# Two chained transformer blocks on one core: gate base product spread over the last two experts, last weight strip in two transfers, memory query copy and compressed maximum reordered

## What is computed

```python
def expert_choice_ffn(h, w_router, w_gate, w_up, w_down):      # 16 experts, 32 rows each
    aff = softmax(h @ w_router);  gates, idx = top_k(aff.T, 32)
    xe = h[idx]
    ye = (silu(xe @ w_gate) * (xe @ w_up)) @ w_down
    return zeros_like(h).at[idx].add(ye * gates)

x = x + expert_choice_ffn(rms_norm(x, norm_ffn), w_router, w_gate, w_up, w_down)
g = sigmoid(rms_norm(x, norm_ple) @ w_ple_gate)
e = rms_norm(p @ w_ple_proj, norm_ple_post)
x = x + g * e
...
# second block, for each of four groups of heads (and, beside it, recurrence head and memory head g)
s = q @ kc.T * NSA_SCALE;  p = masked_softmax(s)               # compressed
s = qh @ k.T * MEM_SCALE;  p = softmax(s);  y_mem = p @ v      # memory
```

## Time and profile before

| | us |
|---|---|
| median of 3 runs | 1643.49 (1643.08 to 1643.61) |
| the profiled execution | 1643.12 |
| its span, first to last instruction | 1641.3 |
| TensorE busy | 1333.6 (81%) |
| VectorE busy | 517.7 (32%) |
| ScalarE busy | 187.1 (11%) |
| GpSimd busy | 41.1 (3%) |
| moved | 518.46 MB, mean 316 GB/s |

### The profile page before, as it was taken

One profiled execution on the slowest core, in us unless ns is written; L12 is line 12 of the kernel. 1 busy time (PEld: TensorE's weight loads), 2 busy tenths in 40 slices (PEclk: granted clock), 3 DMA queues, 4 the chain that ended last, 5 costly groups with the idle time before them and its releaser, 6 DMA issues. The chain is left out here.

```text
span 1641.3 us, 21063 instructions
## 1 busy us (share of the span) xinstructions
PE 1333.6 (81%) x8742; PEld 768.8 (47%) x8742; DVE 517.7 (32%) x1100; ACT 187.1 (11%) x499; POOL 41.1 (3%) x91
## 2 busy tenths in 40 slices
PE   9999676666657666765666679999999999999998
PEld 5553121221113111311122123688888999599953
DVE  3432111111101101100110110445545664467875
ACT  2321010000000000000000000224444000100000
POOL 1100000000000000000000000010000000000001
PEclk9999898888889878987888789999999999999999
DMA  9688999999999999999999999823343441444332
GB/s 400 272 328 364 432 428 431 434 425 432 433 428 433 430 430 436 428 429 434 431 429 428 436 429 426 355 81 120 115 169 137 151 179 67 190 155 154 123 136 101
DMA packets 31493, 518.46 MB, mean 316 GB/s; under 512 B 3524, under 2 KB 4552, under 8 KB 7368
## 3 DMA queue, kind: packets, MB, share of 16 engines
q1 hardware_dynamic: 29360, 514.01, 75.0%
q10 hardware_dynamic: 2072, 3.57, 0.7%
HBM read 515.99 MB, written 1.05 MB: 315 GB/s over the span
## 5 line engine op out<-in xcount | busy, mean ns | idle before, releaser
L1023 PE MATMUL ps<-ring,scr 128*32 128x512 f32 (+3 forms) x3234 | 472.3, 712 | 244.9 <-DMA ring<-in_experts 240.2
L1023 PEld LDWEIGHTS ps<-ring,scr 128*32 128x32 f32 (+2 forms) x3234 | 124.0, 135 | 570.1 <-issue 296.1
L1023 PE MATMUL ps<-turned_T,ring 128*128 128x128 f32 (+1 forms) x1760 | 245.3, 299 | 1.1 <-DVE turned_T L1859 0.8
L1023 PEld LDWEIGHTS ps<-turned_T,ring 128*128 128x128 f32 x1760 | 227.1, 192 | 13.9 <-issue 3.5
L1023 PE MATMUL ps<-scr 128*128 128x128 f32 (+12 forms) x828 | 162.2, 396 | 16.9 <-DVE scr L1988 12.2
L1023 PEld LDWEIGHTS ps<-scr 128*128 128x128 f32 (+4 forms) x828 | 89.9, 176 | 82.1 <-issue 43.5
L1023 PE MATMUL ps<-ring,turned_T 128*128 128x128 f32 (+3 forms) x512 | 127.9, 408 | 0.3 <-DMA ring<-in_w_in 0.3
L1991 DVE TENSOR_TENSOR x<-x,ps 128x512 f32<-128x512 f32 x60 | 41.3, 688 | 196.2 <-PE ps L1023 196.1
L1023 PEld LDWEIGHTS ps<-ring,turned_T 128*128 128x128 f32 x512 | 82.8, 191 | 43.0 <-issue 29.9
L1979 DVE SCALAR_TENSOR_TENSOR scr<-scr,ps 128x512 f32<-128x512 f32 x16 | 11.0, 688 | 282.5 <-PE ps L1023 282.5
L1977 DVE SCALAR_TENSOR_TENSOR scr<-scr,ps 128x512 f32<-128x512 f32 x16 | 11.0, 688 | 225.4 <-ACT scr L799 225.4
(11 more groups left out here) (313 smaller groups left out, 1061.1 us busy)
## 6 DMA issues: line engine op xcount, KB each, us to landing
ring<-in_experts SPq DMA_DIRECT2D x69, 4096.0 KB, 23.1
ring<-in_experts SPq DMA_DIRECT2D x48, 2048.0 KB, 21.2
ring<-in_w_ffn_in SPq DMA_DIRECT2D x11, 2048.0 KB, 7.8
ring<-in_w_merge SPq DMA_DIRECT2D x10, 2048.0 KB, 7.7
ring<-in_w_ffn_down SPq DMA_DIRECT2D x11, 1024.0 KB, 4.8
ring<-in_w_out SPq DMA_DIRECT2D x4, 2048.0 KB, 25.4
ring<-in_w_ml SPq DMA_DIRECT2D x4, 2048.0 KB, 7.6
ring<-in_w_nsa SPq DMA_DIRECT2D x4, 2048.0 KB, 8.0
```

The lines of the kernel that those rows point to most:

```text
L1023: return pe.matmul(o, l, rr, start=start, stop=stop)
```

## The change

1. `PARTS` ends in 1: experts 2 to 13 run in loops, and experts 14 and 15 (`LATE`) are both written out in the manner of expert 15, with `w_down` in four strips of 256 columns. The base product multiplies x before expert 14, and both experts add their 32-row result. Blocks (0,0), (1,0) and (0,1) stand in expert 14 where they stood in expert 15, and block (1,1) stands in expert 15 behind strip 3. The gate weights are issued ahead of strip 0 and behind strip 3 of expert 14.
2. The last strip of expert 15 travels as two transfers of 1 MB, and TensorE waits for the second ahead of the ninth of its 16 matmuls.
3. ScalarE copies the memory query ahead of the first exponentials, and VectorE takes the compressed maximum of the first pair and subtracts it behind the maxima of the first two heads; only the read from PSUM stays ahead.

```diff
-PARTS = (2, 2, 3, 3, 3, 2)
+PARTS = (2, 2, 3, 3, 3, 1)
 LAST = EXPERTS - 1
+LATE = (LAST - 1, LAST)
...
+            for e in LATE:
+                pairs = range(0, 8 if e is LAST else 10, 2)
...
+                for n in range(2 * len(pairs), 12):
+                    dst, src = strip_of(slots[n], e, n)
+                    if (e, n) == (LAST, 11):
...
+                        sp.dma_start(dst[:, lower], lead).then_inc(in_lead, 16)
+                        r.load(slots[n], (dst[:, upper], rest))
+                    else:
+                        r.load(slots[n], (dst, src))
...
-                heads_exp(n4, 0)
                 act.wait_ge(proj_ps, g * 6 + 5)
                 act.activation(qm, bank[7][:, 0:T], ACT.Copy, scale=ML_DH ** -0.5).then_inc(proj_sb, 1)
+                heads_exp(n4, 0)
                 heads_exp(n4, 1)
...
+                if halves:
+                    pe.wait_ge(in_lead, 32)
+                else:
+                    arrived(s, 8 + i, e is LAST)
...
+                    if halves and k == 8:
+                        arrived(s, 8 + i, True)
...
+            for e in LATE:
+                if e is LAST:
+                    pe.wait_ge(x_acc, 4 * LAST)
+                gather(e, sele)
...
+                if e is not LAST:
+                    pe.wait_ge(hT_done, 16)
+                    pe.wait_ge(full[9], 144)
+                    gate_product(0, 0)
+                pe.wait_ge(xe_sb, 2 * e + 2)
+                for n in range(8):
+                    gate_up(slots, n)
+                    if e is LAST and n == 3:
+                        gate_product(1, 1)
+                    if e is not LAST and n == 1:
+                        gate_product(1, 0)
+                    if e is not LAST and n == 3:
+                        pe.wait_ge(full[6], 64)
+                        pe.wait_ge(full[7], 32)
+                        gate_product(0, 1)
...
-                compressed_max(n4, g, 0)
+                compressed_read(n4, 0)
                 head_max(n4, 0)
                 head_max(n4, 1)
+                compressed_max(0)
                 head_probs(n4, 0)
```

More of the change, by code:

```diff
@@ L587, in _ @@
             sp.dma_start(slot[9][:, 0:SLOT], a["w_ple_gate"][0]).then_inc(full[9], 16)
[L588 to L596, removed]
+            for e in LATE:
+                pairs = range(0, 8 if e is LAST else 10, 2)
+                for n in pairs:
+                    s = slots[n]
+                    r.load_two(s, ring[:, s * SLOT:(s + 2) * SLOT], packed["experts"][bass.ds((e * 6 + n // 2) * P, P), :])
+                    if e is not LAST and n == 2:
+                        sp.wait_ge(e_sq, 2)
+                        sp.dma_start(later[:, 0:SLOT // 2], a["w_ple_gate"][1, :, 0:SLOT // 2]).then_inc(full[6], 16)
+                        sp.dma_start(turned_T[:, KC * T:], a["w_ple_gate"][1, :, SLOT // 2:SLOT]).then_inc(full[7], 16)
+                for n in range(2 * len(pairs), 12):
+                    dst, src = strip_of(slots[n], e, n)
+                    if (e, n) == (LAST, 11):
+                        at = SLOT
+                        src = packed["experts"][bass.ds((e * 6 + n // 2) * P, P), :]
+                        lead = src[:, at:at + SLOT // 2]
+                        rest = src[:, at + SLOT // 2:at + SLOT]
+                        sp.wait_ge(r.free[slots[n]], r.rounds[slots[n]])
+                        sp.dma_start(dst[:, lower], lead).then_inc(in_lead, 16)
+                        r.load(slots[n], (dst[:, upper], rest))
+                    else:
+                        r.load(slots[n], (dst, src))
             r.renamed(TAIL)
@@ L792, in _, with expert @@
             e.then_inc(lg_exp, 1)
-            def expert(e):
+            def expert(e, late=False):
                 act.wait_ge(gt_ps, e + 1)
@@ L840, in _ @@
                 experts(4 + b)
-            expert(LAST)
             act.wait_ge(e_sq, 2)
[L845 to L851, removed]
+            for n, e in enumerate(LATE):
+                expert(e, True)
+                for i in range(4):
+                    act.wait_ge(y_ps, 2 * LATE[0] + 4 * n + i + 1)
+                    act.activation(ysb[:, i * T:(i + 1) * T], bank[i % 2][:, 0:T], ACT.Copy).then_inc(y_sb, 1)
+                    if e is LAST and i % 2:
+                        act.wait_ge(x_acc, 4 * LAST + i + 1)
+                        for t in range(NT):
+                            half_squares(3, x, t, i // 2)
+                act.wait_ge(sc_ps, 4 * e + 4)
             for t in range(NT):
@@ L1354, in _, with gate_product, late_y @@
                 experts(2 + n, ROT)
[L1357 to L1362, removed]
+            def gate_product(t, h):
+                for k in range(KC):
+                    mm(bank[4 + 2 * t + h], hT[:, k, t * P:(t + 1) * P], w_gate(h, k), k == 0 and (t, h) != (1, 1), False)
+            def late_y(e, i):
                 s = slots[8 + i]
-                arrived(s, 8 + i, True)
+                halves = (e, i) == (LAST, 3)
+                if halves:
+                    pe.wait_ge(in_lead, 32)
+                else:
+                    arrived(s, 8 + i, e is LAST)
                 tall = slot[s].rearrange("p (k n) -> p k n", k=16)
@@ L1419, in _ @@
[L1419 to L1430, removed]
+            for e in LATE:
[3 more added lines that the diff above has]
+                if e is not LAST:
+                    pe.wait_ge(x_acc, 4 * e)
+                    for h in range(2):
+                        for t in range(NT):
+                            half_turn(x, 4, t, h)
+                gather_turned(e)
+                if e is not LAST:
+                    pe.wait_ge(hT_done, 16)
[12 more added lines that the diff above has]
+                        gate_product(0, 1)
+                h_turned(e, slots)
+                pe.wait_ge(ht_sb, e + 1)
+                for i in range(4):
+                    late_y(e, i)
+                    late_folded(e, i)
+                    ins = late_gates(e, i)
+                ins.then_inc(fold_ps, 1)
+                pe.wait_ge(fold_sb, 5 * (e - LATE[0]) + 5)
+                for t in range(NT):
+                    for h in range(2):
+                        ins = mm(bank[4 + 2 * t + h], gT[64 * h:64 * h + 64, t * P:(t + 1) * P], zsb[64 * h:64 * h + 64, :],
+                                 e is not LAST and (t, h) == (1, 1), e is LAST)
+                        if e is LAST:
+                            ins.then_inc(g_ps, 1)
@@ L2022, in turned_base @@
                         tile_gained(3, 4, t, (h,))
[L2024 to L2035, removed]
+            for n, e in enumerate(LATE):
+                expert(e, True, None if n else turned_base)
+                for i in range(4):
+                    dve.wait_ge(fold_ps, 5 * n + i + 1)
+                    dve.tensor_tensor(yfT[:, 2 * i:2 * i + 2, :], bank[i % 2][:, T:T + 64].rearrange("p (k s) -> p k s", k=2),
+                                      vec[:, GAIN(3) + 2 * i:GAIN(3) + 2 * i + 2].unsqueeze(2).broadcast_to([P, 2, 32]), ALU.mult)\
+                       .then_inc(fold_sb, 1)
+                    dve.wait_ge(sc_ps, 4 * e + i + 1)
+                    o = slice(i * T, (i + 1) * T)
+                    dve.tensor_tensor(x[:, :, o], x[:, :, o], bank[2].rearrange("p (t n) -> p t n", t=NT), ALU.add)\
+                       .then_inc(x_acc, 1)
+                dve.wait_ge(fold_ps, 5 * n + 5)
+                dve.tensor_copy(zsb, bank[3]).then_inc(fold_sb, 1)
             def embedded(t, h):
```

55 lines of the change are left out of this document (20 added, 35 removed).

## The result

| | before | with the change |
|---|---|---|
| median | 1643.45 us (12 runs, 1643.08 to 1644.09) | 1647.80 us (12 runs, 1646.57 to 1648.71) |
| ratio, 95% interval | | 1.0026 (1.0019 to 1.0034) |
| profiled execution | 1643.12, span 1641.3 | 1648.28, span 1646.5 |

The change makes the kernel 4.3 us slower, 0.26%. The forecast was +2.8 us (1,646.3, range 1,641.5 to 1,648.5): the sign was right, the time lies in the range, and the size came out 1.5 us too small, on the other side of the 0.2% bound. It lies outside the range that the forecast gave to its own reading (1,644.8 to 1,647.6): the wider range that holds it reaches so far up because of the fourth rival, which did not happen. The spread between runs grew as well, from 1.0 to 2.1 us.

What follows compares the result with a forecast made beforehand. The expert stream bounds the kernel until the last strip lands, then TensorE's own order. Terms +1.3 (base product), 0 (split strip) and +1.5 (groups) give +2.8 us, a median of 1,646.3 us, range 1,641.5 to 1,648.5.

Steps and rivals of the forecast that it cites:

- its own reading: Whole kernel: the main forecast, +2.8 us to 1,646.3, own range 1,644.8 to 1,647.6; chance 0.47.
- the fourth rival: Expert 15: clock falls for strips 6 and 7 and again for the first down strip; +4.7, 1,648.2 us; chance 0.17.
- The rival of TensorE-bound groups: Four groups: the copy's wait goes and nothing replaces it; groups -2.1, total -0.8, 1,642.7 us; chance 0.15.
- the 0.3 us that VectorE's half wins: Groups: first exponentials could start 0.3 us sooner without the compressed maximum's reduce and add, but now wait behind the copy.
- The fall of the clock: Expert 15, strips 6 and 7: after a 4.4 to 5.2 us hole the pair takes 5.9 us instead of 3.64.
- So no landing moves by my count: Experts 14 and 15: same bytes and a queue that stays filled, so every strip lands when it did before.
- the two signs that the prediction named for a wrong reading of the queue: Experts 14 and 15: wait for strips 2 or 3 gone altogether, or a GB/s drop between 950 and 1,040.
- Expert 14, forecast as ending 992 to 995: Expert 14's own work ends 4 to 7 us behind expert 15's strips 0 and 1; the stream covers it, costing nothing.
- The one without a fall of the clock: Expert 15: hole before strips 6 and 7 shrinks below 2.27 us; seam -0.9, total +0.6, 1,644.1 us; chance 0.13.
- The one on the slower side: Expert 15: a second clock fall puts the first down strip at half clock; +1.9 more, +4.7, 1,648.2 us; chance 0.17.

Runs made afterwards that it cites:

- copy: The kernel before with only ScalarE's reordering, the memory query copied ahead of the first exponentials: 1644.66 us, +1.26, ratio 1.0008.
- seam: The kernel before with the base product over experts 14 and 15 and the last strip in two transfers, groups as before: 1646.27 us, ratio 1.0017.
- unroll14: The kernel before with expert 14 written out in TensorE's program, same instructions, order and transfers: 1644.91 us, ratio 1.0011.
- drop11: The kernel before with base block (1,1) left out, so the output lacks that part of the gate: 1644.27 us, ratio 1.0005.
- fill: The kernel of seam with 20 idle products (4.7 us of TensorE) between strips 5 and 6 of expert 15: 1643.82 us, ratio 1.0004.

## Why the prediction was right, and where it was short

- **Part 3**, forecast +1.5, measured +1.15 alone. The working held step by step: copy at TensorE's product, exponentials 1.3 us later, VectorE's start of the division without slack, 13.65 us where 13.7 was worked out. In four groups the trace has 1.4; the medians 1.15. The rival of TensorE-bound groups fell with *copy*. The working also held what the forecast did not follow up: the 0.3 us that VectorE's half wins were named and then counted as lost behind the copy, and alone they are worth 1.2 us.
- **Part 1**, forecast +1.3, measured +2.9. The fall of the clock was right and rightly sized (5.9 us against 5.97 in seam, 6.38 in the profiled execution of the change). The step that failed is "So no landing moves by my count": in seam expert 15's pair lands 1.9 us later, 0.4 of it the offset of that execution and 1.55 because one share of the stream lags sooner once expert 14 is written out (unroll14). With that term the sum comes out: -0.95 for the block moved out of the way, +2.3 for the clock, +1.55 for the landing are +2.9. The queue did stay full, as was said, and the GB/s did not fall. Of the two signs that the prediction named for a wrong reading of the queue, a drop in GB/s could not show this error. The other came: in the change TensorE has no wait ahead of strips 2 and 3 (both pairs in one row of 7.07 us).
- **Part 2**, forecast 0, measured 0.0 behind Part 1 and 0.1 without it, both within the uncertainty.
- **Expert 14**, forecast as ending 992 to 995. The gathering of expert 15 starts behind it, at 997.10 in the change, since its first down strip's chain ran partly at half clock. TensorE came to strips 2 and 3 at 1,003.2, 0.7 us after they had landed (1,002.5): no harm, but no cover left.
- **The sum.** One term is 1.6 us too small and one 0.35 too large; that the time still lies in the stated range is in part luck, as the result says.
- **The rivals.** The one without a fall of the clock fell with the 6.38 us of the pair. The one on the slower side (a second fall of the clock, on the first down strip of expert 15) did not happen: it takes 1.93 us. Its time, 1,648.2, came near the measured one for another reason. In expert 14 that fall did happen, and was covered.

## What to carry to other kernels

Work that fills an engine's wait for a stream can be worth more than its own length: taking 7.1 us of it away made this kernel no faster, and adding 4.7 us of idle products made the changed one 2.4 us faster. So before a filler is moved, work out the hole that it leaves and what the engine does right behind it. Before an in-order engine's instruction is put ahead of another, compare when each one's operand is ready: the copy's operand was ready 1.0 us after that of the exponentials, and the place between the two readiness times (ahead of the fourth exponential) gave both what they needed.

## What the hardware showed

- TensorE's granted clock stood at half (0.50, 1.2 GHz) from 1,020 to 1,025 after 6.07 us without work (drop11), and a pair of strips took 5.67 us; with work up to 0.49 us ahead of the pair (fill) it stayed at 1.00 (2.4 GHz) and the pair took 3.64. It fell after a wait of 2.13 us as well (unroll14: 0.68 as the mean of 1,010 to 1,015, the pair 5.32 us).
- Writing out one expert in TensorE's program, with the same instructions, moved the landings of transfers by 1.6 us in the trace and cost 1.5 us of time by medians.
- A full queue at a steady 430 GB/s does not fix when a strip lands: single strips came 4.9 us apart, and the last one 6.6. One of a transfer's 16 shares came 1.6 us late and the other fifteen did not.
- Across an instruction transfer of 0.02 MB (1.0 to 1.1 us) the summed delay of a transfer's 16 shares rose by 1.4 to 1.8 us, for each of the 29 such transfers between 900 and 985 us in the fourteen traces.
